# Residual rows kept in DRAM, expert rows added to them by indirect DMAs

## The reference, cut to what matters

```python
x = x + gt1 * mixed
h2 = rms_norm(x, lp['g_norm2']) * (1 + sc2) + sh2
x = x + gt2 * moe(h2, lp['w_router'], lp['b_router'], lp['w_gate'], lp['w_up'], lp['w_down'])
# moe: each token has the top two experts of one group
for e in range(N_EXPERTS):
    hid = jax.nn.silu(h @ w_gate[e]) * (h @ w_up[e])
    out = out + combine[..., e:e + 1] * (hid @ w_down[e])
```

## Time and profile before

| what | value |
|---|---|
| median of 3 runs | 1662.59 us (1655.37 to 1666.16) |
| span of the profiled execution | 1665.8 us |
| TensorE busy | 93% |
| VectorE, ScalarE, GpSimd busy | 54%, 42%, 18% |
| layer 0's expert tiles | about 614 to 826 us |
| layer 1's expert tiles | about 1430 to 1636 us |
| moved by DMA | 337.55 MB |

### The profile page before, as it was taken

How to read it: one execution, slowest core, us unless ns; L and a number is a source line. 1 busy time by engine, 2 the same in 40 slices (tenths; PEclk the granted TensorE clock), 3 DMA queues, 4 the chain that set the end, 5 groups by cost and what they waited for, 6 DMA issues and landing times.

```text
span 1665.8 us, 21787 instructions
## 1 busy us (share of the span) xinstructions
PE 1550.5 (93%) x8180; PEld 1107.1 (66%) x8180; DVE 899.4 (54%) x1723; ACT 700.1 (42%) x1335; POOL 297.8 (18%) x321
## 2 busy tenths in 40 slices
PE   4999999999999989999779999999999999899992
PEld 1777777777787855554456777777777888555561
DVE  1566664455554752455575656543455556344554
ACT  4543554445521313444553455534454132144550
POOL 1001000011101014565200010000111010345640
PEclk9999999999999989999989999999999999999996
DMA  8541205534365379999847212353345253898847
GB/s 339 205 153 58 77 26 189 185 109 161 111 234 219 135 278 400 383 401 346 303 178 270 95 39 77 120 185 126 114 152 204 87 202 127 308 414 336 331 143 286
DMA packets 92376, 337.55 MB, mean 203 GB/s; under 512 B 20960, under 2 KB 21024, under 8 KB 89328
## 3 DMA queue, kind: packets, MB, share of 16 engines
q1 hardware_dynamic: 53136, 197.68, 32.5%
q0 software_dynamic: 38992, 135.86, 22.1%
q10 hardware_dynamic: 144, 2.62, 0.4%
HBM read 351.22 MB, written 47.35 MB: 239 GB/s over the span
## 4 chain that ended last, share of the span: by engine, by line
PE 81%; DMA 8%; DVE 6%; ACT 2%; issue 2%; SPq 1%; POOL 0%; POOLq 0%; ACTq 0%; DVEq 0%
PE ps L1884 16%; PE ps L1886 16%; PE ps L1885 16%; PE ps L2214 6%; PE ps L1876 5%; DMA gu_b<-w_gu,eidx 4%; PE ps L2263 3%; PE ps L2036 3%; PE ps L2018 2%; PE ps L1843 2%; PE ps L1792 2%; PE ps L2096 2%; PE ps L2197 2%; PE ps L2230 2%; PE ps L2070 1%
## 5 line engine op out<-in xcount | busy, mean ns | idle before, releaser
L1884 PE MATMUL ps<-hi,hT_hi 128*128 128x512 f32 x960 | 392.8, 409 | 5.5 <-ACT o_a L1094 3.0
L1886 PE MATMUL ps<-hi,hT_lo 128*128 128x512 f32 x960 | 377.1, 393 | 0.0
L1885 PE MATMUL ps<-lo,hT_hi 128*128 128x512 f32 x960 | 376.3, 392 | 0.0
L1884 PEld LDWEIGHTS ps<-hi,hT_hi 128*128 128x128 f32 x960 | 181.8, 189 | 64.8 <-issue 23.6
L1886 PEld LDWEIGHTS ps<-hi,hT_lo 128*128 128x128 f32 x960 | 181.4, 189 | 40.1
L1885 PEld LDWEIGHTS ps<-lo,hT_hi 128*128 128x128 f32 x960 | 182.2, 190 | 32.4
L890 ACT ACTIVATE hi<-raw 128x1024 fp32r<-128x1024 f32 x106 | 108.4, 1054 | 136.6 <-DMA raw<-w_stream 136.6
L1236 DVE TENSOR_TENSOR lo<-raw,hi 128x1024 fp32r<-128x1024 f32 x106 | 127.5, 1220 | 65.4 <-ACT hi L890 65.0
L1715 DVE TENSOR_TENSOR lo<-raw,hi 128x1024 fp32r<-128x1024 f32 x96 | 112.7, 1221 | 39.7 <-ACT hi L1161 33.9
L2214 PE MATMUL ps<-gu_a,xT 128*64 128x512 f32 x256 | 116.1, 607 | 6.7 <-DMA gu_b<-w_gu,eidx 6.7
L2214 PE MATMUL ps<-gu_b,xT 128*64 128x512 f32 x256 | 116.1, 607 | 0.0
(11 more groups left out here) (312 smaller groups left out, 2880.8 us busy)
## 6 DMA issues: line engine op xcount, KB each, us to landing
raw<-w_stream SPq DMA_DIRECT2D x112, 512.0 KB
raw<-w_gu SPq DMA_DIRECT2D x80, 512.0 KB
raw_m<-w_stream SPq DMA_DIRECT2D x68, 512.0 KB, 5.4
raw<-w_dn SPq DMA_DIRECT2D x40, 512.0 KB
bias_na<-na_bias POOLq DMA_DIRECT2D x32, 384.0 KB, 3.4
sg<-sg_d POOLq DMA_DIRECT2D x8, 1280.0 KB, 9.7
y<-ye_d SPq DMA_DIRECT2D x20, 512.0 KB, 5.2
raw_p<-w_stream SPq DMA_DIRECT2D x16, 512.0 KB, 16.0
```

Of the source, the lines that this page charges most:

```text
L1884: pe.matmul(out, w_hi, m_hi, start=first, stop=False)
L1885: pe.matmul(out, w_hi, m_lo, start=False, stop=False)
L1886: return pe.matmul(out, w_lo, m_hi, start=False, stop=last)
```

## The change

`ye_d`, `x_spill`, `store_rows`, `rows_return`, VectorE's `mix_rows`, `gate_rows` and `add_rows` and ScalarE's `ys` are gone. The residual rows lie in a DRAM tensor `acc[l]` with a row for each token, which for the last layer is the output itself, and 128 spare rows behind them. After the middle of the layer SP writes `x` there. Each expert row is multiplied on VectorE with the slot's weight and with the token's gate, and POOL adds the rows to `acc[l]` by an indirect DMA with addition. The choice between the prompt's gate and the latents' gate is made per slot: `gtm` holds the difference and the latents' gate, `p_slot` is 1 for a prompt token.

```diff
+                def row_gates(n):
                     if n >= 2:
-                        dve.wait_ge(y_stored[n % 2].sem, y_stored[n % 2].at(l, n // 2 - 1))
+                        dve.wait_ge(acc_done.sem, acc_done.at(l, ADDS_BEFORE[n - 1] - 1))
...
+                    return chained(STT(out=ysb[n % 2][:], in0=gtm[:, 0, :], scalar=p_slot[:, c:c + 1], in1=gtm[:, 1, :],
+                                       op0=ALU.mult, op1=ALU.add))
+
+                def ys(n, gated):
+
+                    dve.wait_ge(*down_done(l, n))
+                    after(gated)
+                    c = XD_COL[n]
+                    for j in range(2):
+                        half_row = ysb[n % 2][:, 512 * j:512 * j + 512]
+                        ins = STT(out=half_row, in0=ps[:, 2 + j, :], scalar=w_slot[:, c:c + 1], in1=half_row, op0=ALU.mult,
+                                  op1=ALU.mult)
+                    ins.then_inc(y_dve.sem, 1)
```

```diff
+                def add_rows(n, h=0):
+                    a = ADDS_BEFORE[n] + h
+                    if a == 0:
+                        po.wait_ge(x_parked.sem, x_parked.at(l, 0))
+                    else:
+                        po.wait_ge(acc_done.sem, acc_done.at(l, a - 1))
+                    if h == 0:
+                        po.wait_ge(y_dve.sem, y_dve.at(l, n))
+                    p1 = P if IS_FULL[n] else HALF
+                    c = slice(XD_COL[n], XD_COL[n] + 1)
+                    rows_at = row_h[0:HALF, c] if h else row_i[0:p1, c]
+                    po.indirect_dma_start(acc[l], bass.IndirectOffsetOnAxis(rows_at, 0),
+                                          ysb[n % 2][h * HALF:h * HALF + p1, :], None, bounds_check=ACC_ROWS - 1,
+                                          oob_is_err=True, compute_op=ALU.add).then_inc(acc_done.sem, 16)
...
                     if n >= 2:
-                        store_rows(n - 2)
+                        add_rows(n - 2)
...
-                store_rows(MOE_TILES - 2)
-                store_rows(MOE_TILES - 1)
+                    if n - 2 in PAIR_AT:
+                        add_rows(n - 2, 1)
+                add_rows(MOE_TILES - 2)
+                add_rows(MOE_TILES - 1)
+                add_rows(MOE_TILES - 1, 1)
```

```diff
                 def load_back(l):
...
+                    sp.wait_ge(acc_done.sem, acc_done.at(l, N_ADDS - 1))
                     for t in range(NT):
...
+                        sp.dma_start(x[:, t, :], acc_x[l][:, t, :]).then_inc(x_loaded[t].sem, 16)
...
-            rows_return(DEPTH - 1)
-            load_back(DEPTH - 1)
-            for t in range(NT):
-                sp.wait_ge(x_ready.sem, x_ready.at(DEPTH - 1, t))
-                sp.dma_start(y_out[:, t, :], x[:, t, :]).then_inc(s_out, 16)
-            sp.wait_ge(s_out, 16 * NT)
```

More of the change, by code:

```diff
@@ L75 @@
 PAIR_AT = [n for n in range(MOE_TILES) if not IS_FULL[n]]
+ADDS_BEFORE = [sum(1 if full else 2 for full in IS_FULL[:n]) for n in range(MOE_TILES + 1)]
+N_ADDS = ADDS_BEFORE[MOE_TILES]
+ACC_ROWS = (NT + 1) * P
 XD_COL = [n if kind == "full" else N_FULL + n for kind, n in SCHED]
@@ L198, in program @@
         rc = at("rc", [P, NRC], BF16)
-        tok = at("tok", [P, 2 * NT], F32)
+        tok = at("tok", [P, 2 * NT + 2], F32)
+        gtm = at("gtm", [P, 2, D], F32)
         junk_off = top[0]
@@ L333, in program @@
         ysb = [in_lo("ysb0", [P, D], F32, 12), ysb1]
-        x_spill = nc.dram_tensor("x_spill", [P, NT, D], F32, kind="Internal").ap()
+        acc = [nc.dram_tensor(f"x_acc{l}", [ACC_ROWS, D], F32, kind="Internal").ap() for l in range(DEPTH - 1)] + [y_out]
+        acc_x = [a[0:NT * P, :].rearrange("(t p) d -> p t d", p=P) for a in acc]
         mod_d = nc.dram_tensor("mod_d", [DEPTH, 2, 6 * D], F32, kind="Internal").ap()
@@ L476, in program @@
         ht_lo = Signal("ht_lo", sum(IS_SPLIT))
-        y_act = Signal("y_act", MOE_TILES)
         y_dve = Signal("y_dve", MOE_TILES)
-        y_stored = [Signal(f"y_stored{b}", half[b], 0, 16) for b in range(2)]
-        gathered = [Signal(f"gathered{t}", 5 if t == 0 else 3, 0, 16) for t in range(NT)]
-        x_ready = Signal("x_ready", NT)
+        acc_done = Signal("acc_done", N_ADDS, 0, 16)
+        gtm_loaded = Signal("gtm_loaded", 2, 0, 16)
+        x_loaded = [Signal(f"x_loaded{t}", 1, 0, 16) for t in range(NT)]
         def mslot(e, s):
@@ L642, in _ @@
                 head_pair(3)
+                sp.wait_ge(mod_stored.sem, mod_stored.at(l, 3))
+                for cond in range(2):
+                    sp.dma_start(gtm[:, cond, :], mod_d[l, cond, 5 * D:6 * D].partition_broadcast(P)
+                                 ).then_inc(gtm_loaded.sem, 16)
                 def weights(j, units):
@@ L1056, in qkv @@
                         if b == 1:
-                            if first == 0 and l >= 1:
-                                act.wait_ge(x_spilled.sem, x_spilled.at(l - 1, 0))
                             for t in range(NT):
@@ L1751, in _ @@
                     head_rows(l + 1)
+                dve.wait_ge(gtm_loaded.sem, gtm_loaded.at(l, 1))
+                after(chained(TT(gtm[:, 0, :], gtm[:, 0, :], gtm[:, 1, :], ALU.subtract)))
                 for n in range(MOE_TILES):
@@ L1756, in _ @@
                             moe_lo(SCHED[nxt][1], k)
+                    if n >= 1:
+                        gated = row_gates(n - 1)
                     dve.wait_ge(silu_done.sem, silu_done.at(l, n))
@@ L1778, in _ @@
                             next_lo(w)
-                ys(MOE_TILES - 1)
+                ys(MOE_TILES - 1, row_gates(MOE_TILES - 1))
                 if l + 1 < DEPTH:
@@ L1782, in _ @@
                         next_lo(w)
-                else:
-                    for t in range(NT):
-                        add_rows(t, gate_rows(l, t))
         @blk.tensor
```

131 lines of the change are left out of this document (46 added, 85 removed).

## The result

| | before | changed |
|---|---|---|
| median | 1660.74 us (4 runs) | 1744.33 us (1739.64 to 1747.29, 4 runs) |
| ratio, 95% interval | 1 | 1.051 (1.048 to 1.054) |
| span of the profiled execution | 1665.8 us | 1737.7 us |
| layer 0's expert stage | 197.3 us | 248.8 us |
| last `ysb` of layer 0 to first `hid` of layer 1 | 615.9 us | 607.5 us |

The changed kernel is slower by 84 us; in the profiled executions 71.9, because the one of before was the slowest of its four (1666.16) and the one of the changed kernel the fastest (1739.64). A stage runs here from the start of its first `hid` to the end of its last `ysb` pass. VectorE's timeline of the changed kernel has the four ends (start, us, instruction, idle before it); the same rows of before start at 629.38 and 825.98 (0.74 us), 1442.63 and 1635.79 (0.75).

The account below looks back on a forecast made before the run. The DMA engines and TensorE were taken as both full in the expert stages. Stages +54, end -22, layer 1's start -3 made +29; 1665.8 + 29 - 3.2 = 1691 us, own range 1680 to 1728, 8 in 10 to 1640-1745.

Parts of the forecast that it names:

- signs for the forecast: Layer 0's stage: share near 1, about 230 us long, TensorE's busy time unchanged, its `gu_b` and `hid` waits some 30 us.
- Waits on POOL: Expert stages: each add waits for the one before; priced at nothing beyond the bytes, since earlier gathers still fill the queue.
- Rival (d): Expert stages: the chain of landings becomes the bound, three per 21.4 us period; +117 us, 1755 in all; chance 0.20.
- Bytes: Expert stages: 2304 added rows a layer replace 1280 stored; path grows by 36.1 f - 36.5 us, +54 forecast.
- f = 2.5: Expert stages: an added byte costs 2.5 copied ones, a third of the fixed part showing; +54 us.
- the floor of 2: Expert stages: an added row read twice costs at least two copies; f = 2 gives +36 us there.
- the fixed part: Adding DMA: something fixed, 0.25 us a row, beyond two copies; a third of it was let show.
- f = 4.8: From the trace's one adding DMA, alone: 81 GB/s for a full share against 392; upper end, +137 us in the stages.
- VectorE: 0 forecast: Expert stages: `row_gates` and two `ys` passes add 1.8 us a tile, covered by TensorE's work; 0.
- The end of the kernel: Behind the last `ysb`: two 64-row adds replace store, reload, 15 VectorE passes and output DMA; -22 us.
- The start of layer 1: `x` arrives 1.7 us later, four faster tiles give 7 back, part lost at `raw_m`; -3 us.

Follow-up runs that it names:

- e7: The kernel before, with each store of expert rows waiting for the landing of the store before it; 1681.6 us, +18.5 over before.
- e13: The changed kernel with own rows, one plain copy a tile, each waiting for the landing of the one before; 1657.8 us, 14.3 more than without that wait.
- e6: The changed kernel with empty slots skipped, 1280 added rows a layer in place of 2304; 1717.3 us.
- e2: The changed kernel with every slot's row added to a DRAM row of its own, so no add waits for another; 1692.1 us.
- e3: The changed kernel with a DRAM row of its own for every slot, no chain, and plain copies in place of adds; 1668.2 us.
- e8: The kernel before with each store of expert rows made an adding DMA to distinct rows, no wait added, target seeded at the start; 1699.5 us.
- e1: The changed kernel with its row DMAs made plain copies into the same rows, every wait kept; 1701.9 us.
- e9: The kernel before with the changed kernel's gating on VectorE, rows still stored by one plain DMA a tile to distinct rows, no chain; 1660.8 us.
- e4: The changed kernel with `row_gates` directly ahead of the `ys` passes in place of ahead of `hid`; 1730.7 us.
- e5: The changed kernel with own rows, plain copies, no chain, and a pair's tile sent as one DMA of 128 rows in place of two; 1642.5 us.
- e11: The kernel before with the room for indirect DMA descriptors set to 8192 bytes, as the changed kernel has it; 1662.3 us.
- e10: The changed kernel with a pair's second-half add issued directly behind the first, ahead of the `gu_b` and `dn` gathers; 1746.8 us.
- e12: The kernel before with each store an adding DMA that also waits for the landing of the one before; 1724.8 us.

## Why the prediction was right in direction only

**Right: the direction, and that added rows lengthen the full stages.** The time, 1744.33, came out 53 us over the forecast and outside the forecast's own 1680 to 1728; in the range for 8 in 10 it is by 0.7 us. Of the signs for the forecast none held: the share is 0.89 in layer 0's stage and not near 1, the stage lasts 248.8 us and not 230, TensorE's busy time grew by 12 us, and its wait there is 40.3 us for `hid` and nothing for `gu_b`.

**The step that failed: "Waits on POOL ... I price them at nothing beyond the bytes".** They cost 54.2 us as the chain stands with adds, and 33.7 with copies. The reason given, that gathers issued before still fill the queue while POOL stands, holds for one landing a tile in part (e7 +18.5, e13 +14.3) and not for 26 a layer. Rival (d) had this right: its place (three adds per full-and-pair period), its threshold (18 us in sum; 22.6 and 28.3 were measured) and its signs (share 0.89, just under its 0.9; `row_gates` VectorE's longest waits). Its time, 1755 for 1744, is near by luck: it gave the chain all of 117 us, where the chain takes 40.3 of the stages' 92.2 and terms that it did not have take the rest. Its chance of 0.20 was too low. The evidence for it stood in the earlier trace rows: a landing of 12 us and one of 19.7 in a period of 21.4. It was put aside with "a POOL that stands also shortens the queue". The landings came to 5.5 to 15 us in place of 12 each, and three of them still did not fit.

**Bytes: mis-sized, too high.** Forecast +54 us by f = 2.5, each unit whole on the path. By e6, 29.4 us of the 83.6 go with the adds of empty slots alone. What an added row costs the DMA engines can be read from the software queue's line on the pages of e2 (free adds) and e3 (free copies):

```profile
q0 software_dynamic: 39616, 141.62, 25.7%
```

```profile
q0 software_dynamic: 39616, 141.62, 23.0%
```

25.7% of 1689.4 us less 23.0% of 1666.5 is 50.9 us of all 16 engines, for 4608 rows that cost 48.1 as copies at 392 GB/s: f = 2.1. e8 against before gives 2.0 in the same way. That is the floor of 2 that the prediction believed, with next to nothing of the fixed part showing. And of the 50.9 us only 17.7 came out in the stages (443.1 against 425.4) and 23.9 in the time; in e3 the engines had room, 0.88 and 0.77 of the two stages.

The f = 4.8 of the earlier trace rows came from a wrong yardstick: it set a small add that ran alone against copies under full load. At the end of the kernel an add of 64 rows runs alone, and in e1 a copy of 64 rows in the same place (the changed kernel, then e1):

```profile
1722.39:1727.18 4.79, 0.00 (x0) 0.00 (x0) 0.00 (x0) 0.00 (x0) 1.42 (x1) 0.50 0.45 55
```

```profile
1690.75:1693.99 3.24, 0.00 (x0) 0.00 (x0) 0.00 (x0) 0.00 (x0) 0.90 (x1) 0.63 0.38 81
```

The add makes 122 GB/s for a full share, a factor of 3.2 under the loaded 392 (3.5 forecast), but the lone copy makes only 213: like against like, f = 1.7 to 1.8.

**TensorE's clock: no term.** The prediction took TensorE's busy time as unchanged. It grew by 22.3 us in the two stages, at a mean granted clock of 0.90 and 0.93. How much of each other term below is this loss was not split.

**VectorE: 0 forecast.** The work is nearly free (e9), its place is not: `row_gates` ahead of `hid` costs 15.6 us (e4), since it waits there for the adds. The prediction saw that wait and left it to rival (d).

**No term of its own: the second half.** Two DMAs for a pair's tile, the second behind up to 3 MB of gathers (`gu_b` 2 MB, `dn_a` and `dn_b` 0.5 each), cost 26.1 us even as free copies (e5). The prediction counted the bytes of both, and their places only in rival (d).

The two errors are of opposite sign, bytes too dear and waits at nothing. Stages: 13.2 (one free copy of every slot, `row_gates`) + 21.0 (second half) + 17.7 (addition) + 40.3 (chain) = 92.2, where 54 were forecast, all of it as bytes. The parts hang on the order in which they are taken off: with copies the chain is 31.0. The 13.2 is the least certain, for it stands against before's one trace (20.9 against e11's).

**The end of the kernel: -22 forecast, -11.2 measured.** The chain's end shows why:

```profile
1715.35 6.27 DMA y_out<-ysb,row_i
...
1722.39 4.79 DMA y_out<-ysb,row_i
...
1727.95 1.41 POOL y_out L819
```

Behind the end of the last `ysb` come 2.7 us in which the add of the tile before is still under way, 4.8 to the first half's landing, 0.8 to POOL, 4.8 for the second half, and 5.0 in which the trace shows neither an instruction nor DMA traffic. The forecast had 0.8, 2.5, 0.8 and 2.5. It forgot the third link and that tail, for which no run has a reason, and it took 2.10 us for a store of 64 rows. That last store of before moved nothing (0 GB/s in its window), as a tile of empty slots does:

```profile
1637.39:1639.49 2.10, 0.00 (x0) 0.00 (x0) 0.00 (x0) 0.00 (x0) 0.96 (x1) 1.00 0.03 0
```

A copy of 64 full rows took 3.24 us there (e1) and an add 4.79. So not all of the 12 us of the earlier trace rows over 2.10 is queueing either: part is the data. The Trainium skill (DMA: Bandwidth & Descriptors, Anatomy of one DMA) gives a fixed cost of about 2.0 us and the bytes at 436 GB/s; for 64 rows of 4 KB that is an estimate of 2.6 us. Before's empty store agrees with the fixed part, 2.10; e1's copy took 0.6 us more than the estimate, the add 2.2.

**The start of layer 1: -3 forecast, -8.4 measured.** The parts that were priced came out near it. `x` is read in 3.38 us and ScalarE squares it 16.8 us behind the last `ysb`, 4.0 later than before (12.8; forecast 1.7). Then the tiles come faster, the transposes at 910.81 and 918.37 are 7.56 us apart (forecast 7.7, before 9.46). The loss at `raw_m` that the forecast held against it did not come. By the fifth tile's transposes 4.4 us are gained, and 1.8 more behind the `raw_m` wait; the last 2.2 lie later in the layer, and no run says where from.

```profile
890.88 3.38 DMA x<-x_acc
...
894.35 1.16 ACT y L945 x2
```

```profile
910.81 1.04 PE L1789 MATMUL ps<-ident,y 128*128 128x128 f32 x8
...
918.37 1.04 PE L1789 MATMUL ps<-ident,y 128*128 128x128 f32 x8
```

## What to carry to other kernels

Price a wait for a landing, on an engine that issues other transfers in order, by the landings under load times their number per period, and hold the sum against the period; here three landings of 5.5 to 15 us stood against 21.4. The adds into shared rows were chained, which plain stores to distinct rows did without, and the chain cost far more than the 19.6 us that the shorter ends gave back. A buffer that is emptied by two DMAs waits for the second; moving that one forward did not help as long as it stood in the chain (e10). A wait also costs TensorE's clock behind it. And a unit price has to be taken in the state in which it is used: an add alone against a copy under load gave 4.8, like against like gives 1.7 to 2.1.

## What the runs showed of the hardware

**Price of an adding DMA.** Alone 1.7 to 1.8 times a copy of the same 64 rows by engine time, and 1.48 times by time to landing (4.79 against 3.24 us, e1). Over the whole run, nearly all of them in the loaded stages, 2.0 to 2.1 times by engine time (e8 against before, e2 against e3). To issue one for 128 rows takes POOL 1.62 us in the median, a copy 1.02 (e12 and e7).

**TensorE's clock behind a wait.** The granted clock stood at its lower level, 0.50, behind the wait of 7.93 us at 704.8, and was back at 1.00 in 712 to 716.

**POOL issues indirect DMAs at half speed, and sometimes hardly at all, while VectorE runs `lo` passes back to back.** Before's store of 128 rows takes POOL 1.01 us outside such runs and 1.99 under them; the rows (1.99 and 1.98 us) stand under this one:

```profile
666.63 5.77 DVE L1715 TENSOR_TENSOR lo<-raw,hi 128x1024 fp32r<-128x1024 f32 x5 [0.52 <-ACT hi L1161]
```

At times one issue lasts through the whole run. In the changed kernel three took 6.5 us, in e10 nine took about as long, each under such a run and finished about 0.9 us behind it. e10's timeline:

```profile
754.83 5.76 DVE L1682 TENSOR_TENSOR lo<-raw,hi 128x1024 fp32r<-128x1024 f32 x5
755.07 6.43 POOL L792 DMA_INDIRECT dn_a<-w_dn,eidx  x1 [0.30 <-issue]
```

Not every run does this. Under a like run of the changed kernel two issues went through in 2 us each, and before, with as many such runs, has none over 2.1 us in its stages; what decides is open:

```profile
733.38 5.75 DVE L1682 TENSOR_TENSOR lo<-raw,hi 128x1024 fp32r<-128x1024 f32 x5
```

```profile
733.48 1.98 POOL L776 DMA_INDIRECT xg<-h_d,inv_i  x1 [0.30 <-DVE ysb L1708]
735.76 1.97 POOL L792 DMA_INDIRECT dn_b<-w_dn,eidx  x1 [0.30 <-issue]
```

The Trainium skill (GPSIMD Engine Reference, Specifications) says that GpSimd shares its SBUF interfaces with VectorE and meets contention where a VectorE instruction has two SBUF inputs, as a `lo` pass has; these rows agree, and give the size. How much of the 84 us this is was not measured; the three long issues of the changed kernel kept POOL some 14 us longer than 2 us each would have.
